# Gate and up products of four feed-forward layers, ten of eleven tile pairs by Strassen's scheme

## The reference

```python
def swiglu(h, w_gate, w_up, w_down):
    return (jax.nn.silu(h @ w_gate) * (h @ w_up)) @ w_down

x = x + 0.5 * rmsnorm(swiglu(rmsnorm(x, g[0]), gate[0], up[0], down[0]), g[1])
x = x + rmsnorm(token_mixer_2(rmsnorm(x, g[2]), ...), g[3])
x = x + 0.5 * rmsnorm(swiglu(rmsnorm(x, g[4]), gate[1], up[1], down[1]), g[5])
```

## Time and profile before

| | |
|---|---|
| median of 3 runs | 3659.68 us (3653.72 to 3665.08) |
| the profiled execution's own time | 3651.57 us |
| its span | 3649.8 us |
| PE busy | 3288.0 us, 90% |
| DVE busy | 1492.8 us, 41% |
| ACT busy | 1061.0 us, 29% |
| matmuls at L338, three main groups | 1680 + 1568 + 1568 |

### The profile page before, as it was taken

The page is one execution under the profiler, slowest core; times in us unless marked ns, Lnnn a source line. Parts: engine busy times, 40 slices in busy tenths (PEclk is TensorE's granted clock), DMA queues, the critical chain, the costliest instruction groups (busy, mean ns, idle before and its releaser), DMA issues.

```text
span 3649.8 us, 53714 instructions
## 1 busy us (share of the span) xinstructions
PE 3288.0 (90%) x23844; PEld 2478.5 (68%) x23844; DVE 1492.8 (41%) x2122; ACT 1061.0 (29%) x1666; POOL 172.3 (5%) x167
## 2 busy tenths in 40 slices
PE   6989778887998886999999799999999999799999
PEld 5856667764443333887887478878887887478877
DVE  3356655456121114333334553334333334553333
ACT  3227333221100001222323652223222323652222
POOL 0002212131000000000000000000000000000000
PEclk8999889977999997999999799999999999799999
DMA  6140000113799996232131032222332231032221
GB/s 240 52 159 1 3 4 3 34 66 133 312 390 422 421 422 220 87 99 93 70 110 58 1 104 93 92 93 88 102 103 98 72 110 58 1 104 92 93 93 41
DMA packets 173986, 441.04 MB, mean 121 GB/s; under 512 B 5954, under 2 KB 97852, under 8 KB 149180
## 3 DMA queue, kind: packets, MB, share of 16 engines
q1 hardware_dynamic: 173756, 437.61, 32.4%
HBM read 435.49 MB, written 2.10 MB: 120 GB/s over the span
## 4 chain that ended last, share of the span: by engine, by line
PE 68%; DVE 9%; DMA 7%; ACT 3%; issue 3%; POOL 0%; SPq 0%; DVEq 0%; ACTq 0%; POOLq 0%
PE banks L338 32%; PE banks L2263 5%; PE banks L2889 4%; PE banks L2890 4%; PE banks L2888 4%; DMA ring<-in_exp_w_gate 3%; DMA ring<-in_exp_w_up 2%; PE banks L1466 1%; PE banks L782 1%; PE banks L378 1%; PE banks L334 1%; PE banks L1489 1%; PE banks L769 1%; PE banks L1478 1%; PE banks L1180 1%
## 5 line engine op out<-in xcount | busy, mean ns | idle before, releaser
L338 PE MATMUL banks<-mix_r,ring_r 128*128 128x512 f32 x1680 | 660.2, 393 | 0.0
L338 PE MATMUL banks<-mix_r,ffn_r 128*128 128x512 f32 x1568 | 622.4, 397 | 0.0
L338 PE MATMUL banks<-h_r,ffn_r 128*128 128x512 f32 x1568 | 610.3, 389 | 0.0
L295 DVE TENSOR_TENSOR ring_r<-ring,ffn_r 128x2048 fp32r<-128x2048 f32 (+1 forms) x166 | 354.9, 2138 | 220.6 <-ACT ffn_r L292 220.3
L292 ACT ACTIVATE ffn_r<-ring 128x2048 fp32r<-128x2048 f32 (+1 forms) x166 | 297.5, 1792 | 449.7 <-PE banks L338 440.5
L338 PEld LDWEIGHTS banks<-mix_r,ring_r 128*128 128x128 f32 x1680 | 315.2, 188 | 77.9
L338 PEld LDWEIGHTS banks<-h_r,ffn_r 128*128 128x128 f32 x1568 | 294.4, 188 | 68.4
L338 PEld LDWEIGHTS banks<-mix_r,ffn_r 128*128 128x128 f32 x1568 | 294.4, 188 | 62.3
L2263 PE MATMUL banks<-ring,arena 128*64 128x512 f32 x1120 | 268.1, 622 | 43.0 <-DMA ring<-in_exp_w_gate 17.8
L2889 PE MATMUL banks<-ring_r,ffn_r 128*128 128x512 f32 x704 | 279.3, 397 | 0.0
L2888 PE MATMUL banks<-ffn_r 128*128 128x512 f32 x640 | 250.6, 392 | 4.7 <-DVE arena L2839 4.7
(11 more groups left out here) (451 smaller groups left out, 5174.9 us busy)
## 6 DMA issues: line engine op xcount, KB each, us to landing
ring<-in_exp_w_gate SPq DMA_DIRECT2D x31, 2048.0 KB, 17.6
ring<-in_w_ffn_gate SPq DMA_DIRECT2D x44, 1024.0 KB, 5.4
ring<-in_w_ffn_up SPq DMA_DIRECT2D x44, 1024.0 KB, 8.0
ring<-in_exp_w_down SPq DMA_DIRECT2D x20, 2048.0 KB, 17.7
ring<-in_w_ffn_down SPq DMA_DIRECT2D x20, 2048.0 KB, 7.8
ring<-in_exp_w_up SPq DMA_DIRECT2D x19, 2048.0 KB, 15.0
ring<-in_w_in SPq DMA_DIRECT2D x17, 2048.0 KB, 8.3
arena<-in_exp_w_up SPq DMA_DIRECT2D x13, 2048.0 KB, 17.7
```

What stands on the lines that cost most here:

```text
L295: l.did(V.tensor_tensor(lo, x_, hi, ALU.subtract).then_inc(l.sem, 1), name, "lo", v)
L338: ins = TE.matmul(m[1](bank), m[2], m[3], start=m[4], stop=m[5])
```

## The change

Of the 11 tile pairs of each feed-forward part the first is computed as before. The other ten give 20 products, `v` = 0 to 19 (gate and up of each pair in turn), each a matrix of 256 features x 1024 times 1024 x 512 tokens. Each is cut into quarters: features in two tiles of 128 (left, right), k in two halves of four tiles, tokens in two halves of 256. Strassen's scheme (in the form with seven products and shared sums) then takes seven products of quarters instead of eight:

- Weight sums, all on DVE: S1 = right low-k + right high-k; S3 = left low-k - right low-k (in place); S2 = S1 - left low-k; S4 = left high-k - S2.
- Token sums T1 to T4, once for each feed-forward part: T1 and T3 and T2 on DVE, T4 on POOL, split on ACT and DVE.
- Operands are called E (left tile, both k halves), O (S3 and right high-k), S12 (S1, S2) and S4. Each is split: hi on ACT, lo on DVE. E, O and S12 have 1024 elements a partition, S4 has 512.
- PE runs products 1, 5, 7, 6, 2, 3, 4 (`s_pe`), each 4 k-tiles x 3 matmuls of 256 columns. Products 1, 5, 7 and 6 start a bank each (banks 0 to 3 for even `v`, 4 to 7 for odd). Products 2, 3 and 4 go on in the banks of 1, 5 and 7, once ACT has copied 1 ("P1c") and 5 ("P5c") and DVE has read banks 7 and 6 ("UV").
- Output sums on DVE: UV (512), their sum (256), `outer` (512, "C21"), and for every second `v` a multiply of 256 ("C11") and one of 768. ACT takes Silu (256 and 768) of the gate's result in place of Sigmoid.
- Weights for `v` come as single loads of 1 MB into four half slots; the down weights use two of the ring slots in turn; the fence ahead of the down stage is gone, and `split_down` waits for the last product and the last `hid` instead. PE's first down pair waits for "C21" and "C11" of the last two `v`.

```diff
+                    def sum_dve(l, v, name):
+                        if v >= NU:
+                            return
+                        s1, s2 = s12(v)[:, 0], s12(v)[:, 1]
+                        if name == "S1":
+                            l.wait_ge(*raw_full[v])
+                            old_done(l, v)
+                            ins = V.tensor_tensor(s1, raw(v, 1, 0), raw(v, 1, 1), ALU.add)
+                        elif name == "S3":
+                            l.wait_ge(*past(sx, "S1", v))
+                            ins = V.tensor_tensor(raw(v, 1, 0), raw(v, 0, 0), raw(v, 1, 0), ALU.subtract)
+                        elif name == "S2":
+                            l.wait_ge(*past(sx, "S1", v))
+                            ins = V.tensor_tensor(s2, s1, raw(v, 0, 0), ALU.subtract)
+                        else:
+                            l.wait_ge(*past(sx, "S2", v))
+                            ins = V.tensor_tensor(s4(v), raw(v, 0, 1), s2, ALU.subtract)
...
+                    def dve0(l):
+                        diff_dve(l, "T1")
+                        diff_dve(l, "T3")
+
+                    def then0(l):
+                        diff_dve(l, "T2")
+                        for name in ("S1", "S3", "S2"):
+                            sum_dve(l, 0, name)
+
+                    def act1(l):
+                        diff_hi(l, "T3")
+                        hi_act(l, 0, "O")
+
+                    def dve1(l):
+                        diff_lo(l, "T3")
+
+                    def then1(l):
+                        sum_dve(l, 0, "S4")
+                        lo_dve(l, 0, "E")
+                        lo_dve(l, 0, "O")
...
+                        n_loads[0] = n0 + 4 * (s_ + 2) if s_ % 2 else n0 + 4 * (s_ + 1) + 1
                         downs.append(stream(wd.rearrange("(f p) n -> p f n", p=P)[:, 4 * s_:4 * s_ + m_, :], (m_, D)))
+                        if s_ == 1:
+                            following = (l_, 2) if f_ == 0 else ((1, 0) if l_ == 0 else None)
+                            gain_rows(nm + "g", (l_, 4 * f_ + 1), following, sx)
...
+                    PRODUCTS = {1: ("E", 0, B11, 0), 2: ("E", 4, B21, 0), 3: ("S4", 0, B22, 1), 4: ("O", 4, dparts["T4"], 2),
+                                5: ("S12", 0, dparts["T1"], 1), 6: ("S12", 4, dparts["T2"], 3), 7: ("O", 0, dparts["T3"], 2)}
+                    FREE_BANK = {2: "P1c", 3: "P5c", 4: "UV"}
+                    in_place = lambda v, o, m=1: banks[:, 4 * (v % 2) + o:4 * (v % 2) + o + m, 0:256]
+
+                    def s_pe(l):
+                        for v in range(NU):
+                            for p in (1, 5, 7, 6, 2, 3, 4):
+                                name, k0, (b_hi, b_lo), o = PRODUCTS[p]
+                                if p == 1 and v >= 2:
+                                    l.wait_ge(*past(sx, "C11", v - 2))
+                                elif p == 5 and v >= 2:
+                                    l.wait_ge(*past(sx, "C21", v - 2))
+                                elif p == 1 and v == 0:
+                                    for i in range(4):
+                                        l.wait_ge(*past(nm, "read", i))
+                                elif p == 1:
+                                    l.wait_ge(*past(sx, "T2"))
+                                if v == 0 and p >= 4:
+                                    l.wait_ge(*past(sx, "lo", {4: "T4", 5: "T1", 6: "T2", 7: "T3"}[p]))
+                                l.wait_ge(*past(sx, "lo", v, name))
+                                if p in FREE_BANK:
+                                    l.wait_ge(*past(sx, FREE_BANK[p], v))
+                                _, a_lo, a_hi = operand(v, name)
...
+                        for v in range(NU):
+                            hi_act(l, v + 1, "E")
+                            if v % 2:
+                                silu768(v - 1)
+                            l.wait_ge(*past(sx, "P", 1, v))
+                            if v >= 2:
+                                l.wait_ge(*past(sx, "C21", v - 2))
+                            l.did(S.activation(c51[:, v % 2, 1], in_place(v, 0)[:, 0, :], ACT.Copy).then_inc(l.sem, 1), sx, "P1c", v)
+                            l.wait_ge(*past(sx, "P", 5, v))
+                            l.did(S.activation(c51[:, v % 2, 0], in_place(v, 1)[:, 0, :], ACT.Copy).then_inc(l.sem, 1), sx, "P5c", v)
+                            hi_act(l, v + 1, "O")
+                            hi_act(l, v + 1, "S12")
+                            hi_act(l, v + 1, "S4")
+                            if v % 2 == 0:
+                                l.wait_ge(*past(sx, "P", 2, v))
+                                l.did(S.activation(head256(v), in_place(v, 0)[:, 0, :], ACT.Silu).then_inc(l.sem, 1), sx, "C11", v)
...
+                        def outer(v):
+
+                            c12_21 = sums_of(v)[1]
+                            l.wait_ge(*past(sx, "P", 4, v))
+                            l.did(V.tensor_tensor(c12_21, in_place(v, 1, 2), c51[:, v % 2, 1:2, :].to_broadcast([P, 2, T // 2]), ALU.add)
+                                  .then_inc(l.sem, 1), sx, "C21", v)
...
+                        for v in range(NU):
+                            sum_dve(l, v + 1, "S1")
+                            if v:
+                                outer(v - 1)
+                            sum_dve(l, v + 1, "S3")
+                            sum_dve(l, v + 1, "S2")
+                            if v:
+                                product(v - 1)
+                            sum_dve(l, v + 1, "S4")
+                            lo_dve(l, v + 1, "O")
+                            lo_dve(l, v + 1, "E")
+                            l.wait_ge(*past(sx, "P5c", v))
+                            l.wait_ge(*past(sx, "P1c", v))
+                            l.wait_ge(*past(sx, "P", 6, v))
+                            l.did(V.tensor_tensor(c51[:, v % 2], in_place(v, 2, 2), c51[:, v % 2], ALU.add).then_inc(l.sem, 1), sx, "UV", v)
+                            l.wait_ge(*l.own())
+                            l.did(V.tensor_tensor(sums_of(v)[2], c51[:, v % 2, 0], c51[:, v % 2, 1], ALU.add).then_inc(l.sem, 1))
+                            if v % 2:
+                                l.wait_ge(*past(sx, "C11", v - 1))
+                                l.wait_ge(*past(sx, "P", 2, v))
+                                l.did(V.tensor_tensor(head256(v), in_place(v, 0)[:, 0, :], head256(v), ALU.mult).then_inc(l.sem, 1), sx, "C11", v)
+                            lo_dve(l, v + 1, "S12")
+                            lo_dve(l, v + 1, "S4")
+                            if v == NU - 1:
+                                split_first(l)
+                        outer(NU - 1)
+                        product(NU - 1)
...
+                        l.wait_ge(*past(sx, "used", NU - 2))
...
+                        l.wait_ge(*past(sx, "used", NU - 1))
+                        l.wait_ge(*past(sx, "hid", NU - 1))
```

251 lines of the change are left out of this document (204 added, 47 removed).

## The result

| | before | after |
| --- | --- | --- |
| median of the runs, us | 3657.45 (4 runs) | 3608.3 (4 runs, 3599.99 to 3615.89) |
| profiled execution / its span, us | 3651.57 / 3649.8 | 3615.89 / 3614.1 |
| mean granted clock in that span | 0.944 | 0.931 |

The ratio is 0.9863, with an interval of 0.9832 to 0.9893: 49 us less, where 80 were forecast (3578). The time lies inside the stated range (3562 to 3612), but outside the forecast's own (3566 to 3590): it is inside only because the range also took in most of rivals A and B. The sign and the main term were right; one term of the sum, the start of the stage, was too small by a factor of about four (38 us with what followed from it, against 9).

A forecast was written before the change was run, and what follows sets the result against it. PE's matmuls were taken to bound the feed-forward parts. Terms of -91 + 9 + 0 + 0 + 0 = -82 us on 3651.6 gave 3569.6, as a median 3578; own range 3566 to 3590, stated range 3562 to 3612.

The forecast's parts named there:

- Rival A: In each `v`, DVE is the bound; time 3590 to 3625 us; chance 20%.
- Rival B: Change of stages: T4, first loads or last down pair late by 5 to 10 us a part; chance 7%.
- Term 1: Feed-forward matmuls: 118.5 ns each at 256 columns, 9.95 us a `v`; saves 91 us in four parts.
- Rivals C: Product boundaries: waits ahead of every 12th matmul empty PE's weight-load queue; slower above 0.146 us each; chance 5%.
- D: PE: weight load and matmul run one behind the other, halving columns halves only a part; 4335 us; chance 1%.
- E: PE: the seven products don't replace the eight, other groups stay; chance 1%.
- the rule of the Trainium skill on weight loads: PE: loads overlap running matmuls only where the row group differs; 214 ns a matmul, the change would lose.
- Term 2: DVE in each `v`: 8.7 of PE's 9.95 us, 88% full, keeps up; cost zero, bound 20 us.
- Term 3: Start of the Strassen stage: PE idles 2.3 us behind DVE's queue; 9 us in four parts, bounds 0 to 16.
- Term 4: Start of the down products: PE waits 1.3 us, before 1.34; net zero, within 1 us a part.
- Term 5: Weight loads: 1 MB lands in 5.0 to 8.0 us, covered; taken as zero, 5 us at 8.0 us landing.

The follow-up runs named there:

- all3: Changed kernel with T4 on DVE, PE waiting for one bank at a time, and the down operand's split earlier: 3575.31 us, ratio to before 0.9764.
- sum2: Changed kernel with S1 made twice on DVE in every `v`: 3623.1 us (one run), period of a `v` 9.94 us.
- sum3: Changed kernel with S1 made three times on DVE in every `v`: 3657.56 us (one run), period of a `v` 10.46 us.
- no_t4: Changed kernel with POOL's two T4 sums left out, two memsets in their place: 3582.62 us, ratio to before 0.9799.
- t4_dve: Changed kernel with T4 computed by DVE instead of POOL: 3587.32 us, ratio to before 0.9804.
- bank: Changed kernel where in `v` = 0 each product waits for its own bank alone and 7 goes ahead of 5: 3592.13 us, ratio to before 0.9828.
- early: Changed kernel with the first down operand's split moved ahead of the last `v`'s UV on DVE and to that `v`'s start on ACT: 3605.1 us, ratio 0.9858.

## Why the prediction was partly right

**Term 1, the matmuls: right.** 118.1 ns a matmul, 9.937 us a `v` against 118.5 and 9.95. A wait that is fulfilled costs nothing: seven products a `v`, and behind `v` = 0 no two starts are more than 0.14 us apart. Rivals C, D and E are gone with it, and with D the rule of the Trainium skill on weight loads, as the prediction read it. A wait that is really waited for costs 0.08 us beside its idle time, as bounded (0.07): in all3, at the upper clock, the first matmul behind one records 0.36 us instead of 0.28.

**Term 2, DVE keeps up: right.** Busy 89% of the steady part, idle only behind ACT (before lo O) and PE (before S1), slack 0.7 to 1.46 us by sum2 and sum3, PE never stopped. Rival A is refuted by sum2: with 0.7 us more on DVE the period did not move. DVE's own idle time was 0.8 to 1.2 us a `v` where 0.25 to 0.6 were forecast.

**Term 3, the start of the stage: the step that failed.** The sum over DVE's queue put the end of its last product at 2203.1, 19.0 us behind the first matmul at L334, and the idle time at 2.3. Without POOL's T4 (no_t4) the queue ends at 2176.28, 19.6 us behind that matmul (2156.64), and the idle time is 3.0: the list of DVE operations was right to 0.6 us. With T4 it ends 23.9 behind. The failing sentence is that T4, "made on POOL meanwhile, is needed only by the last product": I asked who waits for T4 and not what T4 takes from its neighbours. Two 2.8 us operations of POOL held back two sums of DVE that lay on the only path of the stage: 4.3 us a part, 17 in all. The bound of 4 us a part in the sum did not contain it, since it was made from DVE's own durations alone. The kernel before already showed the block (L1238 above). Rival B named T4 among six candidates, and its 5 to 10 us a part is about the size that came (7.2: 5.0 of idle time and 2.2 of clock), but its mechanism was lateness, not the block; it had 7%. So that the time lies in the range is in part luck: the range was widened for other reasons than the one that came true.

The second half of the miss is the clock. Behind the 7.2 us idle PE runs at 1.2 GHz for 3.1 to 5.5 us (twelve parts in three profiles), which makes the first `v` 12.1 us instead of 9.94: 2.2 us a part, 8.7 in all. The prediction had reckoned no clock cost behind an idle time at all. It is not the sum of the idle time that decides: 5.4 us in one piece (t4_dve) were followed by the slow clock in all four parts, 5.6 us in four pieces (bank) in none. But pieces are no guarantee: in all3 one part of four fell behind a piece of 2.0 us. At 3.0 us in one piece (no_t4) the first `v` took 10.0 twice, 11.5 and 11.6, so there too it went either way, and what decides in one part was not settled.

The sum for a part: 240.07 - 226.35 = 13.7 us gained against 82 / 4 = 20.5. Missing are 6.8: idle 7.3 instead of 2.3 (5.0), the first `v` (2.2), less 0.3 from a slightly shorter `v`; the rest, 0.1, is rounding. Four parts: 55 gained by the profiles, 49 by the medians, whose interval (0.9832 to 0.9893, 39 to 61 us) contains it.

**Term 4, the down start: right**, 1.08 us idle, 1.24 behind PE's 9.94, forecast 1.3, and removed by moving the split (early). **Term 5, loads: right**, no wait for a transfer in the feed-forward parts; 1 MB lands in 5.1 to 5.5 us.

## What to carry over

When work is given to an engine that stands idle, ask what it reads and who else reads SBUF in that moment, not only who waits for its result: two-input elementwise work on POOL beside DVE work with both inputs in SBUF was not parallel, and the path pays if DVE's operation is on it. The trace of before may already hold the price: look for one operation that has two durations. Where a stage starts behind a queue that is late, let every product wait for its own bank and operand alone: several short idle times kept the clock in seven of eight parts (bank, all3), where one of 5 or 7 us lost it every time. And measure with the stretch between two marks that the change encloses, before reading a median whose rest moves by 10 us.
